# A two-layer decoder trunk on one core: how the kept experts' rows and the far rows of the first tile are joined behind each expert stage

## The reference, cut to what matters

```python
for layer in range(DEPTH):
    mix = conformer_conv(...) if layer < N_CONV_LAYERS else swa_sink_attention(...)
    x = deepnorm(x, mix, ln_g[layer, 0], ln_b[layer, 0])
    ffn = grouped_moe(x, router_w, router_b, moe_w_gate[layer], moe_w_up[layer], moe_w_down[layer])
    x = deepnorm(x, ffn, ln_g[layer, 1], ln_b[layer, 1])

# grouped_moe, per token n with its two experts e0, e1 and normalised gates:
#   y[n] = sum over j of gate[n, j] * (silu(x[n] @ w_gate[ej]) * (x[n] @ w_up[ej])) @ w_down[ej]
```

## Time and profile before

| | us |
|---|---|
| median of three runs (1066.39 to 1067.72) | 1066.97 |
| the profiled execution: its own time | 1069.39 |
| its span, first to last instruction | 1067.7 |
| TensorE busy | 939.2 (88%) |
| VectorE busy | 449.8 (42%) |
| ScalarE busy | 182.5 (17%) |
| GpSimd busy | 184.6 (17%) |

### The profile page before, as it was taken

How to read it: one execution, slowest core, us unless ns; L and a number is a source line. 1 busy time by engine, 2 the same in 40 slices (tenths; PEclk the granted TensorE clock), 3 DMA queues, 4 the chain that set the end, 5 groups by cost and what they waited for, 6 DMA issues and landing times.

```text
span 1067.7 us, 15579 instructions
## 1 busy us (share of the span) xinstructions
PE 939.2 (88%) x6018; PEld 502.8 (47%) x6018; DVE 449.8 (42%) x909; ACT 182.5 (17%) x396; POOL 184.6 (17%) x304
## 2 busy tenths in 40 slices
PE   6999989899997889896688999999999777988994
PEld 4444344566553445452443444555765343544541
DVE  3799973661110112110687456666512121111116
ACT  0000032431111000000223223345311000110000
POOL 1330020213211122100421001021231013021022
PEclk9999999999998999998798899988999899999998
DMA  9994389997999999999750003315699999999953
GB/s 291 379 409 169 78 284 398 378 383 276 367 393 380 424 368 403 374 428 406 253 232 1 0 1 115 122 45 192 246 346 390 377 399 400 384 412 344 411 188 118
DMA packets 75351, 308.70 MB, mean 289 GB/s; under 512 B 9519, under 2 KB 21723, under 8 KB 59130
## 3 DMA queue, kind: packets, MB, share of 16 engines
q1 hardware_dynamic: 37056, 229.53, 56.2%
q10 hardware_dynamic: 28218, 51.93, 13.1%
q0 software_dynamic: 9984, 25.97, 6.9%
HBM read 250.33 MB, written 53.74 MB: 285 GB/s over the span
## 4 chain that ended last, share of the span: by engine, by line
PE 54%; DMA 19%; DVE 17%; issue 5%; ACT 3%; POOL 1%; DVEq 0%; POOLq 0%; ACTq 0%; SPq 0%
PE ps L819 15%; DMA wring<-in_moe_w_up_dram 12%; DVE arena L1186 8%; PE ps L829 7%; PE ps L714 5%; PE ps L1017 4%; PE ps L1036 3%; PE ps L839 3%; PE ps L641 3%; DMA wring<-in_moe_w_gate_dram 3%; DMA arena<-xs_dram 2%; PE ps L849 1%; PE ps L1076 1%; PE ps L1064 1%; PE ps L1090 1%
## 5 line engine op out<-in xcount | busy, mean ns | idle before, releaser
L819 PE MATMUL ps<-wring,arena 128*64 128x256 f32 x1504 | 177.6, 391 | 23.5 <-DMA wring<-in_moe_w_gate_dram 14.9
L819 PEld LDWEIGHTS ps<-wring,arena 128*64 128x64 f32 x1504 | 110.7, 140 | 85.8 <-DMA wring<-in_moe_w_gate_dram 18.5
L641 PE MATMUL ps<-arena,wring 128*128 128x512 f32 x256 | 110.4, 593 | 1.4 <-DVE arena L1144 1.4
L1390 DVE COPY arena<-ps 128x256 f32<-128x256 f32 x32 | 13.6, 425 | 219.1 <-PE ps L927 204.9
L1186 DVE SCALAR_TENSOR_TENSOR arena<-arena,dwT 128x512 f32<-128x512 f32 x145 | 102.3, 781 | 0.0
L2010 POOL DMA_DIRECT2D arena<-xs_dram x112 | 59.5, 538 | 195.1 <-DVE arena L1369 159.4
L1017 PE MATMUL ps<-wring,arena 128*128 128x512 f32 x192 | 87.7, 613 | 3.0 <-ACT arena L1843 3.0
L829 PE MATMUL ps<-wring,arena 128*64 128x512 f32 x384 | 86.6, 592 | 0.6 <-DVE arena L1390 0.6
L641 PEld LDWEIGHTS ps<-arena,wring 128*128 128x128 f32 x256 | 48.5, 190 | 61.9 <-issue 60.3
L819 PE MATMUL ps<-arena 128*64 128x256 f32 x544 | 64.0, 389 | 10.5 <-DMA arena<-in_moe_w_gate_dram 9.7
L1996 POOL TENSOR_TENSOR rstd<-vareps,half 128x1 f32<-128x1 f32 x20 | 23.7, 1187 | 274.2 <-DVE vareps L1203 274.2
(11 more groups left out here) (244 smaller groups left out, 1114.4 us busy)
## 6 DMA issues: line engine op xcount, KB each, us to landing
wring<-in_moe_w_gate_dram SPq DMA_DIRECT2D x23, 2048.0 KB, 25.9
wring<-in_moe_w_up_dram SPq DMA_DIRECT2D x23, 2048.0 KB, 21.1
wring<-in_moe_w_down_dram SPq DMA_DIRECT2D x23, 2048.0 KB, 21.3
xs_dram<-zero ACTq DMA_DIRECT2D x2, 16384.0 KB, 50.9
arena<-in_moe_w_gate_dram SPq DMA_DIRECT2D x9, 2048.0 KB, 21.1
arena<-in_moe_w_up_dram SPq DMA_DIRECT2D x8, 2048.0 KB, 26.9
arena<-in_moe_w_down_dram SPq DMA_DIRECT2D x6, 2048.0 KB, 23.4
xs_dram<-arena ACTq DMA_DIRECT2D x60, 128.0 KB, 8.7
```

The lines of the kernel that those rows point to most:

```text
L641: last = pe.matmul(ps[:, 2 * (c % 4) + h, :], w[:, k, h, (c % 2) * P:(c % 2) * P + P], xT[:, k, :], start=(k == 0), stop=(k == KD - 1))
L819: mm = pe.matmul(ps[h * CAP:(h + 1) * CAP, bank, 0:256], act[:, k, :], w[:, k, h * 256:(h + 1) * 256], start=(k == 0), stop=(k == KD - 1))
```

## The change

- Layer 0 now keeps experts 14 and 15 too, for tile 0 alone (`SUMMED = (1, T)`). `pick(0, ...)` and `turn_picks(0, ...)` run in layer 0 for one tile, in the quarters of a row that is free then.
- Tile 0, in both layers: GpSimd's gathers of tile 0 in layer 0 wait for the stores of experts 0 to 13 only, and for expert 14's weight slot to be free (`s_gud`). VectorE adds the gathered rows to x (`add_far`), then adds TensorE's sum of the two kept experts (`add_kept`). ScalarE scales x of tile 0 by 1.414 in layer 1's stage too.
- TensorE does the kept product of expert 14 between `stage_h(15)` and `stage_y(15)` (`first_kept`), and that of expert 15 behind `stage_y(15)`; `far` of tile 0 is gone. In layer 1 tile 1's product of expert 14 goes first into the wait for expert 15's copy.
- In layer 0 ScalarE stores experts 14 and 15 only after `s_yg[0]` and the copy of 15 (four DMA issues in a row); GpSimd gathers tiles 1 to 3 after that and after tile 0's `inverse_std`. VectorE joins tiles 0 and 1 first, tile 2 after `soft(0, 0)`, tile 3 after `soft(1, 1)`, that is in the loop of t = 1 behind kh = 0. GpSimd's `inverse_std` of tile 3 stands ahead of `scaled_router`, `resrow` and both `residual`s.
- `idle(3, 56)` behind `sums(0)` takes the place of `wait_ge(s_yg[0])` and `idle(0, 32)`.
- Layer 1: GpSimd issues all eight gathers before any `inverse_std`. VectorE does the next tile's sum between x = (x - mean) * g and the wait for 1/std (`meanwhile`).
- SyncE: the first `wo` half waits also for tile 0's norm, the first weights of layer 1 for tile 3's norm.

```diff
-        yg_slots = [(6, 7), (7, 5)]
+        yg_slots = [((3, 0), (6, 0), (5, 0), (5, 1)), ((7, 0), (7, 1), (5, 0), (5, 1))]
...
+        SUMMED = (1, T)
...
             consumed(0, 3 * E - 5)
+            sp.wait_ge(s_ln, T + 1)
             sp.dma_start(slot(3, KD), wo_src[:, :, 0:512]).then_inc(s_wo[0], 16)
...
             consumed(0, 3 * E - 1)
+            sp.wait_ge(s_ln, 2 * T)
             weights(1, 0)
...
+            def kept(l, t, i, start, stop):
+                pe.wait_ge(s_yc, E * (l + 1) - 1 + i)
+                for h in range(2):
+                    part = slice(h * CAP, (h + 1) * CAP)
+                    last = pe.matmul(ps[:, 2 * t + h, :], picksT[l][part, i, t * P:(t + 1) * P], ysb[i][part, :],
+                                     start=start, stop=stop)
+                return last
...
+            def first_kept(l):
+                pe.wait_ge(s_picked, 2 * (l + 1))
+                pe.wait_ge(s_sg, E * (l + 1))
+                kept(l, 0, 0, True, False)
+
+            def sums(l):
+                if l == 1:
+                    pe.wait_ge(s_hTc, E * DEPTH)
+                    kept(1, 1, 0, True, False)
+                kept(l, 0, 1, False, True).then_inc(s_sum, 1)
+                if l == 0:
+                    return
                 pe.wait_ge(s_diag, 1)
...
+                for t in range(1, T):
...
+                    if t > 1:
+                        kept(1, t, 0, True, False)
+                    kept(1, t, 1, False, False)
+                    far(t).then_inc(s_sum, 1)
...
                 stage_h(E - 1, 1)
+                first_kept(l)
                 stage_y(E - 1, 1)
...
-            pe.wait_ge(s_yg[0], 32)
-            idle(0, 32)
+            sums(0)
+            idle(3, 56)
...
                 own(dve.scalar_tensor_tensor(out=xt, in0=xt, scalar=mv[:, n, 0:1], in1=lnrow[:, which, 0, :],
                                              op0=ALU.subtract, op1=ALU.mult))
+                if meanwhile is not None:
+                    meanwhile()
                 dve.wait_ge(s_rs, n + 1)
...
+            def add_far(l):
+                dve.wait_ge(s_xal, T + l)
+                dve.wait_ge(s_yg[0], 32 * (l + 1))
+                for j in range(2):
+                    own(dve.scalar_tensor_tensor(out=x_sb[:, 0, :], in0=yg[l][0][j], scalar=gate_far[l][:, j, 0:1],
+                                                 in1=x_sb[:, 0, :], op0=ALU.mult, op1=ALU.add))
+
+            def add_kept(l):
+                dve.wait_ge(s_sum, l + 1)
+                own(dve.tensor_tensor(x_sb[:, 0, :], x_sb[:, 0, :], ps[:, 0:2, :].rearrange("p a b -> p (a b)"), ALU.add))
...
+                add_far(1)
+                add_kept(1)
+                for t in range(T - 1):
+                    norm_x(t, n + t, 1, 1, meanwhile=lambda: summed(t + 1))
+                norm_x(T - 1, n + T - 1, 1, 1, pieces=2)
...
-            combine(0, n, range(T - 1))
+            combine(0, n, range(2))
...
-                    combine(0, n - T, range(T - 1, T))
+                    combine(0, n - T, range(2, 3))
...
+                    if t == 1 and kh == 0:
+                        combine(0, n - T, range(3, T))
...
+                if l == 0:
+                    act.wait_ge(s_yg[0], 32)
+                    act.wait_ge(s_yc, E)
+                    for b, e in enumerate(KEPT):
+                        send(e, b)
...
-                    pool.wait_ge(s_y[b], 32 * (8 * (l + 1) - l))
+                    pool.wait_ge(s_y[b], 32 * (8 * (l + 1) - l - (l == 0)))
+                if l == 0:
+                    pool.wait_ge(s_gud, E - 1)
...
                 for t in range(T):
+                    if l == 0 and t == 1:
+                        inverse_std(n)
+                        for b in range(2):
+                            pool.wait_ge(s_y[b], 32 * 8)
...
-                    if t >= 2:
-                        inverse_std(n + t - 2)
-                for t in range(T - 2, T):
+                for t in range(l == 0, T):
                     inverse_std(n + t)
```

More of the change, by code:

```diff
@@ new lines, in far @@
+            def far(t):
+                pe.wait_ge(s_yg[t], 32 * DEPTH)
+                for j in range(2):
+                    for h in range(2):
+                        last = pe.matmul(ps[:, 2 * t + h, :], diag[:, j, t, :], yg[1][t][j][:, h * 512:(h + 1) * 512],
+                                         start=False, stop=j == 1)
+                return last
+            def first_kept(l):
+                pe.wait_ge(s_picked, 2 * (l + 1))
+                pe.wait_ge(s_sg, E * (l + 1))
+                kept(l, 0, 0, True, False)
@@ L870, in sums @@
                     if t == 2:
+                        done = pe.snap(g, min_val=1, max_val=4096)
                         pe.wait_ge(s_oyc, done)
[L872 to L889, removed]
@@ L1123, in _ @@
             experts(1)
-            sums()
+            sums(1)
         @block.vector
@@ L1423, in experts, with pick @@
                     step(e, e // 2, e % 2, last=e == E - 1)
-                    if l == 1 and e < 8:
-                        pick(e - 2)
+                    if e < 8:
+                        pick(l, e - 2)
                 copy_h(E - 1, 1, True)
-            def pick(part):
+            def pick(l, part):
                 if part == 0:
-                    dve.wait_ge(s_kept, 1)
+                    dve.wait_ge(s_kept, l + 1)
                 elif part < 3:
-                    for t in range(2 * part - 2, 2 * part):
+                    tiles = range(2 * part - 2, min(2 * part, SUMMED[l]))
+                    for t in tiles:
@@ L1444, in pick @@
-                    dve.tensor_tensor(picks.rearrange("p t i d n -> p (t i) d n"), both[0], both[1], ALU.add
+                    both = [hits[l][:, j, :, :].rearrange("p t (i n) -> p (t i) n", i=2).unsqueeze(2)
+                            .to_broadcast([P, 2 * SUMMED[l], 2, CAP]) for j in range(2)]
+                    dve.tensor_tensor(picks[l].rearrange("p t i d n -> p (t i) d n"), both[0], both[1], ALU.add
                                       ).then_inc(s_picks, 1)
-                else:
-                    for t in range(T):
+                elif l == 1:
+                    for t in range(1, T):
@@ L1825, in _ @@
             experts(0)
-            for t in range(T - 1):
-                gated_y(0, t)
             def take(u):
@@ L1877, in _ @@
                 if i == 1:
-                    gated_y(0, T - 1)
+                    for t in range(SUMMED[0], T):
+                        gated_y(0, t)
             act.dma_start(resrow, attn_bo[0].partition_broadcast(P)).then_inc(s_rows3, 16)
@@ L2066, in _ @@
                 scatter(0, t)
+            number_kept()
             experts(0)
```

92 lines of the change are left out of this document (45 added, 47 removed).

## The result

The changed kernel takes **1053.43 us** in the median of six runs (1052.0 to 1058.62), beside 1066.68 (1063.68 to 1071.81) for six runs of the kernel before on the same chip: ratio 0.9878, 95% interval 0.9845 to 0.9912. It is faster by 1.2%, inside the forecast range, and 4.2 us above the forecast value. The profiled execution took 1058.62 (span 1056.9), the slowest of the six, so its stretches say more than its total. I cut each span at seven instructions that all kernels have. `h0` is the last pair of transposes of layer 0's expert stage (L927 before, L937 after), which the change does not touch; all else is a distance from the mark ahead of it.

What follows compares the result with a forecast made beforehand. Taken as bound: behind layer 0 the wait for expert 15's store and tile 0's gather, behind layer 1 TensorE, then VectorE's joins. -12.6 - 2.1 + 0.5 - 3.6 = -17.8 gave 1049.2 us, range 1045.5 to 1055.

Steps and rivals of the forecast that it cites:

- Boundary, forecast -12.6: Behind layer 0's experts: tile 0's transposes (`Xa`) start at 509.45 instead of 522.07, 12.6 us less.
- the 511 that I had named: Behind layer 0: the forecast counts as wrong if `Xa` waits for tile 0's norm beyond 511.
- I take 6.5: it is the same instruction, and then too the DMA engines were 0.95 busy at 347 GB/s: Tile 0's early second gather behind layer 0: 6.5 us, from 6.47 measured behind expert 15; upper bound 27.8.
- the case that they run too long on a slow clock: Fillers before tile 0's transposes: up to 10 us on the slow clock, ending at 511.6 at worst, 2.2 late.
- 56 take 6.2: Fillers behind layer 0's kept sum: 0.11 us each on a fast clock, from 501.6 to 507.8, under the norm.
- Attention, forecast -1.6: Attention: 2.1 us less in tile 0's heads (bounds 1.3 and 2.9), 0.5 more in tile 1's (0 to 4.9).
- Tail, forecast -3.6: Behind layer 1: first sum 2.9 us earlier, TensorE the bound at 5.57 a tile; 3.6 less (bounds 2.5 and 4.1).
- A: Tile 1's heads: VectorE becomes the bound, 3.3 us lost and 1.6 more in a slow unit; 1053.6 us, chance 0.18.
- B: Behind layer 0: early gather lands by 498.9, so the kept sum decides; 1.5 us less, 1047.7 us, chance 0.12.
- C: Tile 1 comes late, stores and gathers behind the weights, 4 us later overrunning 2 of cover; 1051 us, chance 0.04.
- D: Slower than before: tile 0's gather queues behind weight loads, deciding from 24.3 us after issue; 1070.5 us, chance 0.02.
- E: Tile 0 is early but TensorE waits for Q weights; 1053 us if they come 4 us later still, chance 0.02.

Runs made afterwards that it cites:

- hold3: Changed kernel with the K/V and both Q weight loads held until tile 0's early rows have landed; 1050.82 us, ratio 0.983.
- hold2: Changed kernel with only the two Q weight loads held until tile 0's early rows have landed; 1052.8 us, ratio 0.9892.
- fill96: Changed kernel with 96 fillers instead of 56 behind layer 0's kept sum; 1051.39 us, ratio 0.9835.
- oldtail: Changed kernel with layer 1's joining as it was before the change, layer 0 left as changed; 1056.57 us, ratio 0.989.
- nomean: Changed kernel with the next tile's sum after each last norm instead of inside it; 1056.45 us, ratio 0.9899.
- fill96_mid: Changed kernel with 96 fillers instead of 56, and GpSimd's bias-row scaling and residual 0 ahead of tile 2's 1/std; 1047.65 us, ratio 0.9817.

## Why the prediction was right, and where it was not

**Boundary, forecast -12.6, measured -5.6 up to `KT`: the mis-sized term.** Counted from h0, as the earlier trace rows have it at 494.46, the forecast's steps and the measured ones are: store of expert 13 landed at 491.9, measured 492.6 (488.84 + 8.05 = 496.9, less 4.31); from there to the second gather 2.2, measured 2.2; the gather 6.5, measured 9.08. The additions therefore end at 506.6 instead of 503.4, and `Xa` starts at 512.7 instead of 509.45: past the 511 that I had named as the point at which this step is wrong. The store's landing is 0.7 of these 3.2, the gather 2.6. The step that failed is "I take 6.5: it is the same instruction, and then too the DMA engines were 0.95 busy at 347 GB/s". Two stretches with about equally busy engines needn't price a request alike: behind expert 15 the gather took 6.47; at its new hour, beside the weight loads, 8.86 to 10.34 in all profiles but hold3's, and 5.13 there. The trace of before had a hint: the K/V load had landed at 500.49 and the first query load at 506.85, ahead of the gather at 508.05, and only the second was still in flight, to 512.96; at the gather's new hour all three were. The count alone does not explain it, since in hold2 too a single load was in flight and the gather took 8.86. That the weight loads are the cause is shown; why their packets go first is not, nor why one load does as much as three. The Trainium skill ("DMA: Bandwidth & Descriptors", section "Anatomy of one DMA — SWDGE (gpsimd) path") gives an estimate of 3.2 us for 512 KB, as the forecast worked out. No run shows it: the second gather of tile 0 took 5.13 at the least (hold3), and the shortest of all gathers of this size 4.18 (the first of tile 1, fill96).

**The clock, 3.8 of the lost 7.0.** The forecast had bounded the fillers by the case that they run too long on a slow clock. The reverse was missed: if the norm is 3.2 late, the fillers end 4.55 early and the three units behind run slow. The term "56 take 6.2" was right (6.33); what hung on it was not costed. Both errors have one root, the gather, since hold3 removes both with the same 56 fillers, up to its late query load. With a gather of 5.1 `Xa` came 14.26 behind h0, where the forecast with 6.5 had 14.99: the other steps to `Xa` held, but for the store that landed 0.7 later.

**Attention, forecast -1.6, measured -5.3.** In tile 0 the mechanism was right and its size too small: the wait fell by 1.2 (taken: 0.8), the unit by 1.56 (taken: half of 1.6), and 0.8 came from the heads behind (taken: 0.5). That is 3.56 for the 2.1 of the forecast, and above its upper bound of 2.9. In tile 1 GpSimd's price was 1.23, in the third head, above the 0.5 taken and far below the 4.9; that it cost that stage nothing in sum is owed to the clock, since tile 2's K/V unit took 7.10 where before it took 8.89 (at 593.62): the granted clock was 1.00 under it (588 to 595) and 0.50 before (593 to 597), behind an idle stretch of much the same length (3.67 and 3.79). The last 1.07, in the router stage, is scatter of the clock: the run repeated has it 0.7 longer than before, and gains 4.1 in the three stages. The Trainium skill's rule on the port pair that VectorE and GpSimd share, which one of the two holds for a whole instruction ("SBUF — State Buffer", section "SBUF: two separate sides"), held in all runs. VectorE operations of 0.15 to 0.42 us took 2.3 to 2.6, wherever GpSimd's work was put.

**Tail, forecast -3.6, measured -3.74.** Right in mechanism and size: first sum 6.75 behind expert 14's kept product (forecast 6.6), TensorE the bound at 5.55 per tile (5.57), VectorE waiting 0.2. oldtail and nomean confirm both parts.

**Rivals.** A: the wait in tile 1's heads is there, at 1.23 instead of the 3.3 that it needed. B: the gather was slower, not faster; even hold3's additions end at 503.14 (500.54 and 2.60), 0.8 after the kept sum, so the kept sum decided in none of these runs. C: tile 1's rows landed in time, no TensorE wait stands for them. D: 9.08 is far from 24.3. E: no wait for the query weights in the change; but hold3 shows how thin that cover is, since loads issued at 501.5 were 2.31 late.

The total landed within range because the errors partly cancel: the boundary gained 7.0 less than forecast, attention 3.7 more, the tail 0.1 more. That leaves 3.2 of the 4.2 between forecast and median; the last 1.0 is within the scatter. So the range was met partly by luck: with attention as forecast the boundary alone would have brought the time to about 1056, above the 1055 of the range. The range's lower end was also added up 0.4 too low: -12.6, -1.5, -2.9 and -4.1 from 1066.97 give 1045.9, not 1045.5.

## What to carry to other kernels

A small transfer that is put ahead of a wait has to be priced in the company it will have there: look for what else is queued at that hour, since 2 MB loads in flight turned 5.1 us into 9, with the engines about as busy (1.00) as where 6.5 had been read (0.95). Fillers that hold TensorE's clock must reach the start of the real work, and their number belongs to the longest wait seen, not to the expected one: 56 that ended 4.55 us early were worth no more than 8. GpSimd work on SBUF is best moved to an hour in which VectorE has slack, which can matter more than how long it takes.

## What was not expected of the hardware

- The early gather (512 KB, 128 rows of 4 KB, second of two) took 5.1 us with no weight load in flight, 8.9 to 10.3 with one to three 2 MB loads in flight, whether these had been issued ten us before it or one. In the changed kernel its queue moved 2 packets of 320 from 498 to 502 us.
- After 4.55 us of idle TensorE the granted clock stood at 0.50 for the next five us and more, and three units took 23.88 instead of 20.84; after 0.83 or 0.60 us it stayed at the fast level. Time gained at the fast level was given back in one profile (fill96, a unit of 8.89 and tiles 1 to 3 longer by 2.0) and kept in another (fill96_mid). What decides between them stays open.
- The same kernel reached h0 at 492.55 in one execution and at 498.77 in another, and all profiles of kernels that are alike up to there lie from 492.5 to 498.8. So a few us between single executions say little, which is why stages were compared.
